# Attention stage of a hybrid transformer layer on one core: probabilities transposed two key tiles at a time, and the low products of two score chunks side by side on TensorE

## The reference, cut to what matters

```python
s = jnp.einsum('bqkgd,bskd->bkgqs', qi, k_all).astype(jnp.float32) * (HEAD_DIM ** -0.5)
p = jax.nn.softmax(s, axis=-1).astype(v_all.dtype)
return jnp.einsum('bkgqs,bskd->bqkgd', p, v_all)
```

## Time and profile before

| what | us |
|---|---|
| median of 3 runs | 2033.14 (2031.74 to 2034.86) |
| the profiled execution | 2035.89 |
| its span | 2033.3 |
| PE busy in the span | 1856.9 (91%) |
| DVE busy | 1614.0 (79%) |
| ACT busy | 1303.5 (64%) |

### The profile page before, as it was taken

One profiled execution on the slowest core, in us unless ns is written; L12 is line 12 of the kernel. 1 busy time (PEld: TensorE's weight loads), 2 busy tenths in 40 slices (PEclk: granted clock), 3 DMA queues, 4 the chain that ended last, 5 costly groups with the idle time before them and its releaser, 6 DMA issues.

```text
span 2033.3 us, 28027 instructions
## 1 busy us (share of the span) xinstructions
PE 1856.9 (91%) x8691; PEld 1462.4 (72%) x8691; DVE 1614.0 (79%) x2070; ACT 1303.5 (64%) x1921; POOL 290.0 (14%) x294
## 2 busy tenths in 40 slices
PE   6998869899899889719999999999999999999996
PEld 3776647666666666517888888888888888888884
DVE  5777547766766767487989998999899989998996
ACT  4444347666766766416777777777777777777774
POOL 0233221110111111101101100110011001110113
PEclk8999879999999999958999999999999999999998
DMA  8556480210110120039999999999999999999996
GB/s 353 172 151 170 109 228 28 63 41 22 62 44 28 52 62 10 31 120 365 396 394 390 376 377 402 389 381 370 405 386 384 368 404 386 373 384 398 380 379 245
DMA packets 108034, 512.28 MB, mean 252 GB/s; under 512 B 12064, under 2 KB 36040, under 8 KB 57296
## 3 DMA queue, kind: packets, MB, share of 16 engines
q1 hardware_dynamic: 101792, 489.11, 63.7%
q0 software_dynamic: 4752, 17.30, 3.2%
q10 hardware_dynamic: 1440, 5.24, 0.7%
HBM read 481.71 MB, written 27.28 MB: 250 GB/s over the span
## 4 chain that ended last, share of the span: by engine, by line
PE 54%; DVE 2%; DMA 1%; issue 0%; ACT 0%; POOL 0%
PE banks L1599 34%; PE banks L1624 17%; PE banks L1611 1%; PE banks L1580 1%; DVE topi L1458 1%; DVE top L1456 1%; DVE cand L1459 1%; DMA xe<-h_scratch,icol 0%; DVE raw L1554 0%; DMA out<-raw 0%; DVE ysc L1518 0%; DVE ysc L1561 0%; ACT d_hi L1421 0%; POOL out L1381 0%; DVE x_lo L1484 0%
## 5 line engine op out<-in xcount | busy, mean ns | idle before, releaser
L1490 DVE TENSOR_TENSOR w_lo<-raw,w_hi 128x2048 fp32r<-128x2048 f32 x256 | 574.8, 2287 | 67.9 <-ACT w_hi L1399 67.9
L1399 ACT ACTIVATE w_hi<-raw 128x2048 fp32r<-128x2048 f32 x256 | 470.8, 1919 | 10.5 <-DMA raw<-in_w_exp 10.4
L1599 PE MATMUL banks<-w_hi,x_hi 128*128 128x512 f32 x1024 | 406.2, 397 | 1.4 <-DVE x_lo L1484 1.4
L1599 PE MATMUL banks<-w_hi,x_lo 128*128 128x512 f32 x1024 | 400.6, 391 | 0.0
L1599 PE MATMUL banks<-w_lo,x_hi 128*128 128x512 f32 x1024 | 400.1, 391 | 0.0
L1498 DVE TENSOR_TENSOR d_lo<-raw,d_hi 128x1024 fp32r<-128x1024 f32 x256 | 296.2, 1218 | 1.5 <-ACT d_hi L1421 1.4
L1421 ACT ACTIVATE d_hi<-raw 128x1024 fp32r<-128x1024 f32 x256 | 258.1, 1060 | 38.5 <-DMA raw<-in_w_exp 24.7
L1058 DVE TENSOR_TENSOR ptl<-banks,pth 128x384 fp32r<-128x384 f32 x320 | 176.6, 555 | 66.8 <-ACT pth L995 61.5
L995 ACT ACTIVATE pth<-banks 128x384 fp32r<-128x384 f32 x320 | 156.9, 490 | 109.3 <-PE banks L1168 101.1
L1599 PEld LDWEIGHTS banks<-w_hi,x_lo 128*128 128x128 f32 x1024 | 192.9, 188 | 40.7
L1599 PEld LDWEIGHTS banks<-w_hi,x_hi 128*128 128x128 f32 x1024 | 193.2, 189 | 39.7 <-DVE x_lo L1484 1.8
(11 more groups left out here) (213 smaller groups left out, 2768.4 us busy)
## 6 DMA issues: line engine op xcount, KB each, us to landing
raw<-in_w_exp SPq DMA_DIRECT2D x384, 1024.0 KB, 8.0
a_ring<-in_w_mod SPq DMA_DIRECT2D x32, 512.0 KB, 5.0
qt<-q_scratch SPq DMA_DIRECT2D x64, 192.0 KB, 3.6
a_slot<-in_w_mod SPq DMA_DIRECT2D x8, 1024.0 KB, 12.0
a_w_raw<-in_w_in SPq DMA_DIRECT2D x3, 2048.0 KB, 30.2
q_scratch<-a_qst SPq DMA_DIRECT2D x16, 384.0 KB, 3.9
a_xt<-in_x ACTq DMA_DIRECT2D x8, 512.0 KB, 6.1
xr<-in_x SPq DMA_DIRECT2D x8, 512.0 KB, 4.0
```

What stands on the lines that cost most here:

```text
L1399: act.activation(w_hi[which][c][:, :], raw[which][c][:, :], ACT.Copy).then_inc(s["hi_done"], 1)
L1490: dve.tensor_tensor(w_lo[which][c][:, :], raw[which][c][:, :], w_hi[which][c][:, :].bitcast(F32), ALU.subtract).then_inc(s["lo_done"], 1)
L1599: i = pe.matmul(psum[:, 2 * (j % 2) + which, :], x_[par][:, k, :], w_, start=(k == 0 and w_ is hi and x_ is x_hi), stop=(k == KD - 1 and x ...
```

## The change

1. **Slots.** A new helper `batch` puts two items into slot 0 and up to two into slot 2, and none into slots 1 and 3. The transposes of both items come first, and the products of two items earlier follow behind them both. On ACT the two copies, and on DVE the two splits, follow each other in the same slots. The spreading matmul (line 1190) and the output projection's pieces now stand between the transposes and the products.
2. **Low products.** The second matmul of chunks 0 and 1 no longer spans 128 partitions. Both are issued in slot 1: the low query times the high keys of chunk 0 on partitions 0 to 63, and the low query times the high keys of chunk 1 on partitions 64 to 127, into two different banks. For the second one the high keys 512 to 1023 are copied to partitions 64 to 127 of a new tile `kx`, with one transfer at the end of stage A; it lies where `f_tok` lay. Low times low is left out for these two chunks; chunk 2 stays as it was.
3. **Maxima.** As the scores of chunk 0 are whole only in slot 1, DVE takes the maxima of chunks 0 and 1 there, one after the other. In slot 0 it has only splits.

```diff
@@ -125,13 +125,15 @@
         K = ExitStack()
         ks = sb("ks", [P, NKV, KEYS], F32R, K)
         vs = sb("vs", [P, TS, NKV, 2, HD], F32R, K)
+        f_at = nc.sbuf_base
         f_tok = sb("f_tok", [P, TL, FW], F32, K)
-        unit_in, y_t = nc_phase_a(nc, sem, a, psum, ident, ones, eps_c, ks, vs, f_tok, q_d, mod_d, x_d, ctx_d, w_mod, w_in)
+        kx = nc.alloc_sbuf_tensor_at("kx", [P, NKV, UC], F32R, offset=f_at)
+        unit_in, y_t = nc_phase_a(nc, sem, a, psum, ident, ones, eps_c, ks, vs, f_tok, kx, q_d, mod_d, x_d, ctx_d, w_mod, w_in)
         sb("y_hold", [P, 2 * N + 16], F32, K)
         rows = ctx.enter_context(nc.sbuf_tensor("rows", [P, 4, D], F32, side="right"))
         aff = ctx.enter_context(nc.sbuf_tensor("aff", [E, N], F32, side="right"))
         cand = ctx.enter_context(nc.sbuf_tensor("cand", [EH, N // 2], F32, side="right"))
-        nc_phase_b(nc, ctx, sem, sb, a, K, psum, ident, ones, rows, aff, cand, eps_c, ks, vs, y_t,
+        nc_phase_b(nc, ctx, sem, sb, a, K, psum, ident, ones, rows, aff, cand, eps_c, ks, kx, vs, y_t,
                    q_d, mod_d, h2_d, acc_d, x_d)
         K.close()
         nc_phase_m(nc, ctx, sem, sb, a, psum, ident, rows, cand, eps_c, h2_d, acc_d, out_d, out_rows, unit_in)
@@ -279,11 +281,17 @@
                     row_store(n - 1)
                 if n >= 2:
                     store(n - 2)
+                if n == TL + 1:
+
+                    sp.wait_ge(s["pm_done"], 2)
+                    sp.wait_ge(s["k_out"], 64 * TL)
+                    sp.dma_start(kx[HD:P, :, :].bitcast(F32), ks[0:HD, :, UC:2 * UC].bitcast(F32)).then_inc(s["kx_in"], 16)
                 if n < TL:
                     load(4 * n + 3)
             sp.wait_ge(s["row_out"], 16 * TL)
             sp.wait_ge(s["q_out"], 32 * TL)
             sp.wait_ge(s["k_out"], 64 * TS)
+            sp.wait_ge(s["kx_in"], 16)
 
         @block.gpsimd
         def _(pool):
@@ -862,6 +870,10 @@
         lo, hi = ((0, 4), (4, 7), (7, 10))[i % 3]
         return [KT * g + k for k in range(lo, hi)]
 
+    def batch(its, c):
+
+        return its[c:c + 2] if c % 2 == 0 else []
+
     def behind(t, i, prev, cur):
 
         if i == 0:
@@ -986,8 +998,7 @@
                                 act.activation(oth[0:HD, :], psum[HD:P, OB, 0:REP * P], ACT.Copy).then_inc(s["oth_done"], 1)
                             else:
                                 act.activation(oth[HD:P, :], psum[0:HD, OB, 0:REP * P], ACT.Copy).then_inc(s["oth_done"], 1)
-                        if c < len(its):
-                            k = its[c]
+                        for k in batch(its, c):
                             n = NT * t + k
                             act.wait_ge(s["t_done"], n + 1)
                             if not (isinstance(t, int) and t == 0 and k < 4):
@@ -1043,17 +1054,16 @@
                 for i in range(NQ):
                     its = items(i, prev, cur)
                     for c in range(NCH + 1):
-                        if cur and c < NCH:
-                            lo, hi = CH[c]
-                            dve.wait_ge(s["s_done"], NS * t + NCH * i + c + 1)
-                            ins = dve.tensor_reduce(mx[:, i, c:c + 1], psum[:, (NCH * i + c) % 4, 0:hi - lo], AX, ALU.max)
+                        for j in ((), (0, 1), (2,), ())[c] if cur else ():
+                            lo, hi = CH[j]
+                            dve.wait_ge(s["s_done"], NS * t + NCH * i + j + 1)
+                            ins = dve.tensor_reduce(mx[:, i, j:j + 1], psum[:, (NCH * i + j) % 4, 0:hi - lo], AX, ALU.max)
                         if cur and c == NCH - 1:
                             chain(ins)
 
                             chain(dve.tensor_reduce(mx[:, i, 3:4], mx[:, i, 0:3], AX, ALU.max))
                             dve.tensor_scalar(nb[:, i:i + 1], mx[:, i, 3:4], -SCALE, None, ALU.mult).then_inc(s["nb_done"], 1)
-                        if c < len(its):
-                            k = its[c]
+                        for k in batch(its, c):
                             dve.wait_ge(s["hi_done"], NT * t + k + 1)
                             dve.tensor_tensor(ptl[:, k % 4, :], psum[:, PTB + k % 2, 0:REP * P], pth[:, k % 4, :].bitcast(F32),
                                               ALU.subtract).then_inc(s["lo_done"], 1)
@@ -1150,13 +1160,17 @@
                                 pe.wait_ge(s["exp_done"], NS * t + n - 3)
                             o = psum[:, n % 4, 0:hi - lo]
                             pe.matmul(o, qt[:, i, 0, :], ks[:, i // 3, lo:hi], start=True, stop=False)
-                            pe.matmul(o, qt[:, i, 1, :], ks[:, i // 3, lo:hi], start=False, stop=True).then_inc(s["s_done"], 1)
+                            if c == 1:
+
+                                pe.matmul(psum[:, (n - 1) % 4, :], qt[0:HD, i, 1, :], ks[0:HD, i // 3, 0:UC], start=False, stop=True).then_inc(s["s_done"], 1)
+                                pe.matmul(o, qt[HD:P, i, 1, :], kx[HD:P, i // 3, :], start=False, stop=True).then_inc(s["s_done"], 1)
+                            elif c == 2:
+                                pe.matmul(o, qt[:, i, 1, :], ks[:, i // 3, lo:hi], start=False, stop=True).then_inc(s["s_done"], 1)
                         if c == 0 and i in fl:
                             k0 = KT * (fl[i] + 1)
                             times(k0 - 2)
                             times(k0 - 1)
-                        if c < len(its):
-                            k = its[c]
+                        for k in batch(its, c):
                             n = NT * t + k
                             g, kt = k // KT, k % KT
                             if kt in (0, 4, 8):
@@ -1168,8 +1182,13 @@
                                 ins = pe.transpose(psum[:, PTB + k % 2, r * P:(r + 1) * P],
                                                    pr[(g % 2) * 3 + r][:, kt * P:(kt + 1) * P], ident[:, :])
                             ins.then_inc(s["t_done"], 1)
-                            if kt >= 2:
-                                times(k - 2)
+                        if c == 0 and i in fl:
+                            G = 4 * t + fl[i]
+
+                            pe.wait_ge(s["diag_done"], G + 1)
+                            misc_free(f"R{i}")
+                            pe.matmul(psum[:, MB, 0:REP * P], ones[:, :], diag[fl[i] % 2][:, :, :].rearrange("p r n -> p (r n)"),
+                                      start=True, stop=True).then_inc(s["misc_mm"], 1)
                         if prev and cur and i in (4, 5):
 
                             j = i - 4
@@ -1182,13 +1201,9 @@
                             ins = out_part(j, (2 * c, 2 * c + 1), c == 0, c == NCH)
                             if c == NCH:
                                 ins.then_inc(s["misc_mm"], 1)
-                        if c == 0 and i in fl:
-                            G = 4 * t + fl[i]
-
-                            pe.wait_ge(s["diag_done"], G + 1)
-                            misc_free(f"R{i}")
-                            pe.matmul(psum[:, MB, 0:REP * P], ones[:, :], diag[fl[i] % 2][:, :, :].rearrange("p r n -> p (r n)"),
-                                      start=True, stop=True).then_inc(s["misc_mm"], 1)
+                        for k in batch(its, c):
+                            if k % KT >= 2:
+                                times(k - 2)
                     if not cur and i in (4, 5):
                         pe.wait_ge(s["mix_done"], 4 * t)
                         out_part(i - 4, LATE, False, True).then_inc(s["misc_mm"], 1)
```

6 lines of the change are left out of this document (3 added, 3 removed).

## The result

| kernel | median (range), us | ratio to before [95% interval] |
|---|---|---|
| before | 2032.44 (2030.83 to 2034.86) | 1 |
| changed | 2070.31 (2067.39 to 2071.96) | 1.0183 [1.0169, 1.0198] |

The changed kernel is slower by 37.9 us; the forecast was 28 us slower. The profiled execution took 2071.96 us with a span of 2070.0.

The account below looks back on a forecast made before the run. DVE's list with the loop through bias, exponential and copy bounds most heads, PE heads 4 and 5. Terms of 3.5 plus 0.4 for switches make 3.9 us a step, about 28 in all: 2061 us, range 2038 to 2080.

Parts of the forecast that it names:

- heads 4 and 5: Heads with the output projection, bound by PE: a 0.2 us wait in head 4 against 0.23 gained in head 5, together 0.
- heads 0, 10 and 11: Tails from first split to end of bias grow: 0.67 in head 0, 0.45 each in 10 and 11, 0.2 back in 10.
- switches: Changes between 128 and 64 partitions on PE: 0.07 us each, up to 0.16, six on the path, 0.4 a step.
- Maxima behind the splits: DVE idle some 0.7 us before slot 0's first split; tails become 2.97 us, or 3.45 with osum.
- Two items at a time: Same PE instructions, but the second item's transposes wait for the split behind the bias; 0 together with heads 4 and 5.
- The pair: Two low products on PE start together, saving one 512-column pass of 0.23 us a head; bounds 0 to 0.23.
- Heads 3 and 9: Tails with osum grow from 3.16 to 3.45 us, 0.29 in each head.
- The clock: A granted clock below 1.00 in whole steps would come on top of the forecast; no size given.
- Step 0: PE's 8.0 us wait for POOL hides earlier losses; five heads behind lose about 0.4 each, 2 us.
- PE is the bound, the kernel gets faster: Rival, chance 0.13: the saved pass shows in full, 9 to 22 us faster, median 2015 us.
- The pair does not overlap, or the switches drain: Rival, chance 0.14: low products save nothing and switches cost 0.16 each; 2074 us, or 2081 with longer waits.
- Nothing changes: Rival, chance 0.05: half the tails' growth is taken back and PE's saving shows in half the heads; 2034 to 2038 us.

Follow-up runs that it names:

- filler: Changed kernel with six more 512-column matmuls on PE at the end of head 11, ahead of the wait for the affinities: 2062.85 us, ratio 1.0157.
- the order alone: Kernel before with chunk 0's low product, still a whole pass, and its maximum moved to slot 1; single items, no pair: 2067.28 us, ratio 1.0165.
- on the same half: Changed kernel with both low products of slot 1 on partitions 0 to 63, one after the other: 2075.2 us, ratio 1.0205.
- whole passes and items in twos: Changed kernel with the pair of low products replaced by two whole passes over 128 partitions: 2062.49 us, ratio 1.0137.
- `lg` earlier: Reciprocal and scaling of lg on DVE moved to the end of slot 0 of head 11: 2018.24 us on the kernel before, 2055.35 on the changed one.

## Why the prediction was right, and where it was not

The sign and the mechanism were right, and the size of a step was 4.4 us in place of 3.9. That it came so near is partly luck: 0.9 us that were missing in heads 4 and 5 stand against 0.7 too much in heads 0, 10 and 11. To set the terms against measurements I take the time from one bias to the next on DVE, the median of five steps, of the kernel before and of the one with the filler, which has the changed order at a clock of 1.00:

| heads | before | filler | grown | forecast |
|---|---|---|---|---|
| 0 | 6.84 | 7.23 | 0.39 | 0.67 |
| 1 | 4.22 | 4.96 | 0.74 | 0.65 |
| 2 | 3.75 | 4.50 | 0.75 | 0.59 |
| 3 | 5.36 | 5.86 | 0.50 | 0.29 |
| 4, 5 | 17.35 | 18.28 | 0.93 | 0 |
| 6 | 8.29 | 8.66 | 0.37 | 0.44 |
| 7, 10, 11 | 15.53 | 15.74 | 0.21 | 0.57 |
| 8 | 4.53 | 4.53 | 0 | 0 |
| 9 | 6.01 | 6.50 | 0.49 | 0.29 |
| sum | 71.88 | 76.26 | 4.38 | 3.50, and 0.4 for switches |

- **Maxima behind the splits.** Right, and shown by the order alone: +35 us with no instruction more. The hole was forecast at 0.7 us and is 0.72. By windows, undisturbed steps go from 71.88 to 76.14 by this order with single items, and from 72.62 to 75.49 with items in twos.
- **Two items at a time.** I forecast 0. It is 0.74 us a step alone (71.88 to 72.62); beside the order it gives back 0.65 (76.14 to 75.49).
- **The pair.** Overlap right: 0.22 measured for 0.23. **The switches were mis-sized.** I took 0.07 each, 0.16 as the other bound; that row was of seven one-column matmuls at a granted clock of 0.50, and said nothing of a 512-column one at 1.00. In head 2 the pair's row is 0.04 longer than two passes, so with the 0.22 saved the way to 64 partitions and back costs 0.26: 0.08 on the way in (0.32 in place of 0.24), as the row had it, and 0.18 on the way out (0.43 in place of 0.25). In head 5, where the projection's pieces follow, it is more (0.43 + 1.42 for the pair and the four pieces against 0.23 + 1.32 for a pass and the four, so 0.3 for the way out). The rule of the Trainium skill that I had set against my row (TensorEngine Tiling (Array Packing), Key Properties: a change of tiling mode drains the engine) would have made it 0.32, my row 0.14, and 0.26 is nearer to the rule. The trace doesn't show a whole drain: at both switches the next matmul starts 0.07 to 0.08 us before the modelled end of the last. Nor is all of it the switch: two half passes on the same half, with no switch between them, start 0.34 apart.
- **Heads 4 and 5** are the step that failed: 0 forecast, 0.93 measured. I set a saved pass of 0.23 a head against a wait. In head 5 the pass saved in slot 0 was no gain: the projection's first piece waits there for DVE to have read the output bank (0.15 us, line 1099), and the low product had covered that wait. From the first score matmul of the head to that piece it is 1.60 us before and 1.60 by the order alone. Order alone costs each of the two heads 0.23 to 0.25, and the pair adds 0.16 to 0.18 to each. In head 4 the second item's transposes wait 0.63 us for the split behind the late bias, where I had 0.16; of that, 0.12 shows in the head's length (7.48 with whole passes and items in twos, 7.36 by the order alone).
- **Heads 0, 10 and 11** were over-sized: 0.39, 0.04 and 0.28 where I had 0.67, 0.25 and 0.45. Part of the late bias is taken back in the wait at the turn of the step, which I had not counted: with that wait gone (`lg` earlier, with and without the change) head 0 grows by 0.59 and head 11 by 0.47. Head 7, with ACT's square, came as forecast (-0.12 for -0.13).
- **Heads 3 and 9** were under-sized, 0.50 and 0.49 for 0.29: the tail of head 3 is 3.64 and not 3.45. What makes it longer isn't worked out.
- **The clock.** Named as what would come on top, and left out of the sum: 4.7 us of the change's growth. With 30.7 for seven undisturbed steps that makes 35.3 of the 37.9 us between the medians; the rest lies outside the seven steps or in the scatter of the executions (the two profiled ones differ by 36.1). Step 0, for which I had 2 us, brought none that can be seen (59.4 before, 57.9 after, and 57 to 66 over all runs).
- **The arithmetic.** 3.9 us in seven steps and 2 in step 0 are 29, not 28.
- **`kx`.** 0, as forecast.
- **The rivals.** "PE is the bound, the kernel gets faster" falls: PE's busy time did not fall by the 2.8 us that I had given as a sign either: with the earlier `lg` it is 65.8 in a step against 64.9. The order alone, with not one instruction more, already has 66.1 against 65.0, so that figure does not measure PE's work. "The pair does not overlap, or the switches drain" was half right: the first half is false, and what the half passes and switches cost together takes all the gain. "Nothing changes" falls.

## What to carry to other kernels

When two engines pass a loop between them, look at what fills the gap behind the value that closes it: an instruction there costs nothing, and the same instruction behind the gap costs most of its time, without any engine doing more: a maximum of 0.61 us cost 0.37 to 0.41 in heads 1, 2, 7 and 10 by the order alone. A packed pair of matmuls has to be counted with the way into and out of the other tiling, and with its first result coming later than that of a whole pass (0.81 us behind the high matmul here, against 0.63). And look at the turn of a loop for a short instruction queued behind a long chain that it doesn't depend on: moving two of them was worth 14 us here.

## What the runs showed of the hardware that was not expected

- Two 64-partition matmuls of 512 columns on the same half start 0.34 us apart, two over 128 partitions 0.23 (rows of the two kernels above). Of the 0.26 us that the half passes cost in the row of 0.98, 0.11 are between them, 0.08 ahead and 0.07 behind.
- Behind a wait of 1.6 us on PE the granted clock was 0.50 for 3.4 to 6.8 us in six of seven cases, and with six matmuls in that wait it stayed at 1.00 in all seven: worth 7.5 us, which the profiles show as shorter steps at full clock. Taking the wait away was worth more, 15 us, the clock included.
